# Delta-rule layer on one core: ScalarE's decays behind the copy of the state, its first taps of the values behind the next rounding

## The chip, the cores and the metric

The kernel runs on one core of a Trainium2 chip. The metric is the device time of one execution in microseconds, as the median of several runs. One profiled execution gives the trace; times "at 1205" and the like are microseconds from the start of its span. The engines: TensorE (PE in the rows; PEld are its weight loads), VectorE (DVE), ScalarE (ACT), GpSimd (POOL) and SyncE (SP), which issues the loads of the weights. Each runs its own instructions in order and waits on semaphores.

## What is computed

The reference is a block of two layers (one of retention, one of the gated delta rule, each beside an attention to a memory), followed by a second block of pooling, HGRN and an MLP, for 256 tokens of width 2048 in float32. The change touches the layer of the delta rule alone:

```python
qkv = silu(conv4(h[..., :CONV_CH], conv_w))       # causal, 4 taps
q, k = l2_normalised(qkv[...]), ...               # 12 heads of 128; v has 24
beta = sigmoid(b); g = -exp(a_log) * softplus(a + dt_bias)
g_cum = cumsum(g)                                 # over a chunk
decay = tril(exp(g_cum[i] - g_cum[j]))
lower = strict_tril((k * beta) @ k.T * decay)
u, w = solve(I + lower, [v * beta, k * beta * exp(g_cum)])
# per chunk, in order of time:
v_new = u_i - w_i @ state
out = q_i @ state + (q_i @ k_i.T * decay) @ v_new
state = state * exp(g_last) + k_tail.T @ v_new
```

The kernel computes it with two chunks of 128 tokens, called tile 0 and tile 1. So there is one state to be carried over, from tile 0 to tile 1, and it starts from zero.

## The kernel before

**Units and halves.** Nearly all the work of TensorE is products of the activations with weights that stream in from memory. They are cut into units of 2048 x 512 weights (or 512 x 2048 for the output), and a unit into 8 halves, q = 0 to 7, of 256 x 512. To keep float32's precision on TensorE each half is split in a high part `whi`, which ScalarE rounds (`half`, line 1080), and a low part `wlo = raw - whi`, which GpSimd computes in two instructions (line 440). TensorE then does 12 matmuls on the half (lines 496 to 498). There are four buffers for halves: ScalarE rounds half q only when TensorE has done half q-4, and GpSimd and TensorE follow in order. GpSimd does nothing but this.

**A group of the delta rule.** The layer runs over 6 groups of 4 value heads (2 heads of q and k). A group has a unit for q and k, one for v, one for the gate z, and from group 1 on one for the output projection of the group before. Groups 2 to 5 stand in a loop of two bodies; groups 0 and 1 are written out ahead of it, group 0 without the output's unit and with its later steps spread over its z unit in another way (`first_places`).

**Steps.** Everything that isn't a weight product is placed between the halves. After each half q of a unit, ScalarE calls `gdn_steps(g, n, ...)` for the numbers n that belong there: in the unit of q and k first n = 32 + q of the group before, then n = q of this group (`in_qk`); in the unit of v 40 + q and 8 + q; in the unit of z 48 + q and 16 + q (`in_z`); in that of the output 24 + q. TensorE has numbers of the same kind and its own steps (`gdn_run`, `gdn_v`, `gdn_level_p`). ScalarE is three to four halves ahead of TensorE, so the same number doesn't mean the same time. VectorE runs one list without halves.

**What stands around the first move.** In the unit of q and k of group g:
- n = 36 (q = 4) of group g-1: ScalarE scales tile 0's new values (`vn0`, line 1477), which TensorE uses for tile 0's output (`o0`).
- then, still behind q = 4, the decays of group g (lines 1409 to 1421): eight ACTIVATEs with Abs, a drain, and one Exp, for which the activation table is loaded anew. They write `dn`, and end with the semaphore `decay_ready`. VectorE uses them in `gdn_decay` (line 2043) and for the lower triangles.
- n = 37 (q = 5) of group g-1: the copy of the state out of PSUM (`copy_out` of "st", line 1131), which TensorE's next step needs (`from_state`, line 741), and `out_squares(g-1, 0)` (line 1386), which first waits for VectorE's gate of tile 0 (line 2144).
- n = 39 (q = 7): the copy of tile 1's new values; n = 40 and 41 in the unit of v: `out_squares(g-1, 1)` and, behind the next half, the square root of the mean squares (line 1488), which waits for VectorE's line 2175; n = 42: the scaling of the output (line 1493).

VectorE, in the same stretch: tile 0's gate (2144), the new values with the state (2150), tile 1's sum and gate (2157 to 2162), seven small copies of the next group's parameters (2028, 2035 to 2037), `gdn_decay` (2043), the mean squares (2175), the reciprocal (2172), then the turning of q and k (1862).

**Around the second move.** In the unit of z, n = 18: ScalarE copies v out of PSUM (`wide_out`), TensorE turns it (line 555, `gdn_v`), n = 21 (q = 5): `first_tap` of both halves of v (line 1373) starts the convolution, which VectorE goes on with (line 2018) after `gdn_lower` (lines 2051 to 2089) and a small copy (2121). n = 22 (q = 6): `merge` of the triangles for the levels of the inverse. VectorE's `gdn_base` (2097 to 2116) ends the triangles' base with line 2111, and TensorE's first level (line 712) waits for that. In group 0 n = 21 stands behind the z unit's half 4 and n = 22 behind half 5.

Of the kernel before, what the change touches and what calls it, by code (L numbers as in the profile page):

```python
# [119 lines left out]
def fill(phase, step, g=0):  # L120

    for bank in range(4):
        before = 0
        for name, rounds, steps in PHASES:
            if name == phase and step in steps[bank]:
                return bank, g * len(steps[bank]) + (before + steps[bank].index(step) + 1)
            before += rounds * len(steps[bank])
    raise KeyError((phase, step))
# [29 lines left out]
def build(nc, x_in, mem_in, pos_in, w_ret, ret_g, w_gdn, conv_w, a_log, dt_bias, gdn_g, w_kv, w_out,  # L158
# [6 lines left out]
    with ExitStack() as ctx:  # L165
# [906 lines left out]
        def _(act):  # L1072
# [35 lines left out]
            def wide_out(m, pair, func, dst, norm=None, taken=None):  # L1108

                act.wait_ge(sub_used, 8 * m + 8)  # L1110
                if taken is not None:
                    act.wait_ge(wide_taken, 2 * taken)
                for t in range(TT):
                    scale = 1.0 if norm is None else inverse_rms(norm)[:, t:t + 1]
                    act.activation(dst(t), acc[pair][t][:, :], func, scale=scale).then_inc(wide_taken, 1)
# [4 lines left out]
            def tiles(buf):  # L1120
                return lambda t: buf[:, t * COL:(t + 1) * COL]
# [220 lines left out]
            def is_first(g):  # L1342
                return isinstance(g, int) and g == 0
# [23 lines left out]
            def first_tap(dst, tile, step, g):  # L1367

                b, n = fill("gdn", step, g)
                act.wait_ge(filled[b], n)  # L1370
                for k in range(2):
                    c = slice(((tile + k) % 4) * SEQ, ((tile + k) % 4 + 1) * SEQ)
                    op = act.activation(dst[:, c], bank[b][:, k * SEQ:(k + 1) * SEQ], ACT.Copy,
                                        scale=small[:, 88 + tile + k:89 + tile + k])
                return op
# [25 lines left out]
            def gdn_steps(g, n, at, pair):  # L1401
                if n == (8 if is_first(g) else 0):
# [3 lines left out]
                        act.wait_ge(s["decay_ready"], g)  # L1406
                    src = log_decays[:, ds(4 * g, 4), :].partition_broadcast(P)
                    act.dma_start(cb[:, 0:1024].rearrange("p (t h c) -> p t h c", t=TT, h=4), src).then_inc(s["rows_here"], 16)
                if n == (11 if is_first(g) or isinstance(g, int) and g == 1 else 4):
                    if not is_first(g):  # L1410
                        b, c = fill("gdn", "n64", g - 1)
                        act.wait_ge(filled[b], c)
                    act.wait_ge(s["rows_here"], 16 * g + 16)
                    for t in range(TT):
                        for hh in range(4):
                            c = slice(t * COL + hh * P, t * COL + (hh + 1) * P)
                            at_g = TT * NVH + t * NVH + hh
                            bias = gates[:, at_g:at_g + 1] if is_first(g) else gates[:, ds(4 * g + at_g, 1)]
                            act.activation(dn[:, c], cb[:, c], ACT.Abs, scale=-1.0, bias=bias)
                    act.drain()  # L1420
                    act.activation(dn[:, :], dn[:, :], ACT.Exp, scale=-1.0).then_inc(s["decay_ready"], 1)
# [21 lines left out]
                if n == 18:  # L1443
# [1 line left out]
                        b, c = fill("gdn", "o1", g - 1)  # L1445
                        act.wait_ge(filled[b], c)
                    wide_out(at + 1, 1 - pair, ACT.Copy, tiles(n1), taken=W_GDN + 3 * g + 1)
                if n == 21:
                    first_tap(sq, 4, "va", g).then_inc(s["conv_begun"], 1)
                    first_tap(sq, 6, "vb", g).then_inc(s["conv_begun"], 1)  # L1450
                if n == 22:
# [176 lines left out]
            def gate_sums(q):  # L1628
# [11 lines left out]
                act.activation(gates[:, 4 * n48:5 * n48], n1[:, 288:336], ACT.Exp).then_inc(s["gate_step"], 1)  # L1640

            layer(U_GDN, W_GDN, B_L1, gdn_steps, "gdn", "att1", gate_steps, spread_first=True)
            act.wait_ge(s["branch_ready"], 2 * BR)
            ln_rows(1)
# [1079 lines left out]
```

## Time and profile before

| | |
|---|---|
| median of 3 runs | 2769.76 us (2769.64 to 2771.84) |
| profiled execution, its own time | 2771.87 us |
| its span | 2770.1 us |
| TensorE busy | 2742.0 us (99%) |
| GpSimd busy | 2342.9 us (85%) |
| ScalarE busy | 1380.4 us (50%) |
| VectorE busy | 1301.9 us (47%) |
| TensorE's granted clock, mean | 0.997 of 2.4 GHz |

The layer of the delta rule with its attention lies at about 860 to 1690 us of the span; the group that is looked at most runs from 1192 to 1300. A line of a timeline gives the start, the length, engine, line, operation, what it writes and reads, and in brackets how long the engine was idle before it and what ended that. "x6" after the shapes means that six such instructions are merged in one row. Busy times of TensorE are modelled at their ends, so it is the starts of its matmuls that are compared.

### The profile page before, as it was taken

The numbers are of one execution on the slowest core, as the hardware profiler recorded it, in microseconds if no ns is written. First come the engines' busy times: TensorE is split into PE (matmuls) and PEld (weight loads), VectorE is DVE, ScalarE is ACT, GpSimd is POOL, SyncE is SP. The second block draws the span as 40 slices with busy tenths as digits, with TensorE's granted clock in tenths as the row PEclk, the third lists the DMA queues.
The fourth block names the chain that finished last, engine by engine and source line by source line (L and its number), as shares of the span: only waits on it lengthen the run. The fifth ranks groups of instructions, "written<-read, shape, count | busy, mean of one in ns | idle before, by whom it ended". The sixth has DMA issues, their size and how long they took to land.

```text
span 2770.1 us, 38752 instructions
## 1 busy us (share of the span) xinstructions
PE 2742.0 (99%) x12719; PEld 2280.6 (82%) x12719; DVE 1301.9 (47%) x2729; ACT 1380.4 (50%) x1843; POOL 2342.9 (85%) x1831
## 2 busy tenths in 40 slices
PE   8999999999999999999999999999999999999998
PEld 7888888888888888888888887888878888888886
DVE  5232234224663576856757465646253323233234
ACT  4444444444444665665655545655445444444444
POOL 8988898888889867876877787888789999999997
PEclk9999999999999999999999999999999999999999
DMA  8555565555566544554545455555556556565653
GB/s 287 189 185 184 186 198 186 182 186 172 178 228 196 174 140 160 170 161 157 168 159 167 152 175 190 168 167 181 180 169 196 184 194 197 185 198 192 197 189 130
DMA packets 284354, 502.67 MB, mean 181 GB/s; under 512 B 18021, under 2 KB 68662, under 8 KB 283190
## 3 DMA queue, kind: packets, MB, share of 16 engines
q1 hardware_dynamic: 275606, 482.55, 53.4%
q10 hardware_dynamic: 8608, 18.24, 1.8%
q8 instruction: 89, 1.46, 0.2%
q14 instruction: 51, 0.42, 0.0%
HBM read 498.61 MB, written 2.12 MB: 181 GB/s over the span
## 4 chain that ended last, share of the span: by engine, by line
POOL 54%; PE 24%; issue 21%; POOLq 1%; DVE 0%; DVEq 0%; ACT 0%
POOL wlo L440 54%; PE acc L496 8%; PE acc L498 8%; PE acc L497 8%; POOLq L438 0%; POOLq L435 0%; DVE x_sb L2510 0%; DVE big L2486 0%; POOLq L440 0%; DVE kv L1914 0%; DVEq L165 0%; ACT small L1502 0%; DVE small L2477 0%; POOL eps_sb L434 0%; DVE small L2503 0%
## 5 line engine op out<-in xcount | busy, mean ns | idle before, releaser
L440 POOL TENSOR_TENSOR wlo<-raw,whi 128x512 fp32r<-128x512 f32 x1824 | 2342.4, 1316 | 410.0 <-ACT whi L1080 393.6
L1080 ACT ACTIVATE whi<-raw 128x1024 fp32r<-128x1024 f32 x910 | 958.3, 1060 | 1076.2 <-PE acc L498 1034.8
L496 PE MATMUL acc<-whi,a_lo 128*128 128x512 f32 x2528 | 999.5, 395 | 3.1 <-POOL wlo L440 2.4
L498 PE MATMUL acc<-whi,a_hi 128*128 128x512 f32 x2528 | 984.9, 390 | 0.0
L497 PE MATMUL acc<-wlo,a_hi 128*128 128x512 f32 x2528 | 984.3, 389 | 0.0
L496 PEld LDWEIGHTS acc<-whi,a_lo 128*128 128x128 f32 x2528 | 474.9, 188 | 103.4 <-POOL wlo L440 4.4
L498 PEld LDWEIGHTS acc<-whi,a_hi 128*128 128x128 f32 x2528 | 474.4, 188 | 100.1
L497 PEld LDWEIGHTS acc<-wlo,a_hi 128*128 128x128 f32 x2528 | 475.0, 188 | 96.4 <-issue 1.4
L496 PE MATMUL acc<-whi,b_lo 128*128 128x512 f32 x928 | 365.5, 394 | 0.0
L498 PE MATMUL acc<-whi,b_hi 128*128 128x512 f32 x928 | 361.3, 389 | 0.0
L497 PE MATMUL acc<-wlo,b_hi 128*128 128x512 f32 x928 | 361.3, 389 | 0.0
L1914 DVE TENSOR_TENSOR kv<-acc,kv 128x512 f32<-128x512 f32 x160 | 103.2, 686 | 415.9 <-PE acc L498 415.9
L1862 DVE STREAM_TRANSPOSE bank<-br 32x256 f32<-32x256 f32 (+1 forms) x544 | 235.4, 438 | 10.3 <-issue 2.3
L498 PEld LDWEIGHTS acc<-whi,b_hi 128*128 128x128 f32 x928 | 174.2, 188 | 36.5
L497 PEld LDWEIGHTS acc<-wlo,b_hi 128*128 128x128 f32 x928 | 174.4, 188 | 34.8
L496 PEld LDWEIGHTS acc<-whi,b_lo 128*128 128x128 f32 x928 | 174.4, 188 | 34.7
L1914 DVE TENSOR_TENSOR x_sb<-acc,x_sb 128x512 f32<-128x512 f32 x128 | 82.5, 685 | 159.3 <-PE acc L498 159.3
L462 PE MATMUL acc<-whi,a_hi 128*128 128x512 f32 x192 | 79.5, 414 | 2.1 <-ACT a_hi L1143 1.8
L463 PE MATMUL acc<-wlo,a_hi 128*128 128x512 f32 x192 | 77.5, 404 | 0.0
L1814 DVE TENSOR_TENSOR a_lo<-bank,a_hi 128x512 fp32r<-128x512 f32 x32 | 20.7, 685 | 88.8 <-ACT a_hi L1140 88.8
L1961 DVE TENSOR_TENSOR big<-bank,big 128x256 f32<-128x256 f32 x12 | 5.1, 425 | 112.3 <-PE bank L615 111.9
L470 PE MATMUL acc<-whi,a_lo 128*128 128x512 f32 x192 | 52.0, 393 | 0.0
(307 smaller groups left out, 2007.7 us busy)
## 6 DMA issues: line engine op xcount, KB each, us to landing
raw<-in_w_in_ret SPq DMA_DIRECT2D x176, 512.0 KB, 4.4
raw<-in_w_in_gdn SPq DMA_DIRECT2D x176, 512.0 KB, 4.3
raw<-in_w_out SPq DMA_DIRECT2D x160, 512.0 KB, 4.5
raw<-in_w_mlp_in SPq DMA_DIRECT2D x128, 512.0 KB, 4.4
raw<-in_w_mlp_out SPq DMA_DIRECT2D x128, 512.0 KB, 4.3
raw<-in_w_in SPq DMA_DIRECT2D x80, 512.0 KB, 4.5
raw<-in_w_mem_kv SPq DMA_DIRECT2D x63, 512.0 KB, 4.8
cb<-log_decays ACTq DMA_DIRECT2D x6, 512.0 KB, 5.1
```

The source lines that it names most:

```text
L440: part = pool.tensor_tensor(wlo[q % 4][:, c], raw_half[:, c], whi[q % 4][:, c].bitcast(f32), ALU.subtract)
L462: pe.matmul(acc[pair][t][:, :], a_hi[:, at:at + P], w_h, start=start and block == 0, stop=False)
L463: pe.matmul(acc[pair][t][:, :], a_hi[:, at:at + P], w_l, start=False, stop=False)
L470: mm = pe.matmul(acc[pair][t][:, :], a_lo[:, at:at + P], w_h, start=False, stop=stop and block == KB - 1)
L496: pe.matmul(dst, l, w_h, start=start and block == 0, stop=False)
L497: pe.matmul(dst, h, w_l, start=False, stop=False)
L498: mm = pe.matmul(dst, h, w_h, start=False, stop=stop and block == KB - 1)
L1080: act.activation(whi[q % 4][:, :], raw[j][:, (q % 2) * HALF:(q % 2 + 1) * HALF], ACT.Copy).then_inc(hi_ready, 1)
L1814: op = tt(lo, b[:, :], hi, SUB)
L1862: last = dve.transpose(squares(dst, "b t")[32 * j:32 * (j + 1), blocks, :, 32 * i:32 * (i + 1)], squares(src, "t b")[32 * i:32 * (i + 1), ...
L1914: tt(to, acc[(pair + j) % 2][t][:, :], to, ADD).then_inc(out_added, 1)
L1961: tt(pi[:, to:to + SEQ], b[:, 0:SEQ], dec, MUL)
```

## The change

Two numbers in `gdn_steps` of ScalarE. The decays of group g move from behind half 4 (and n = 36 of the group before) to behind half 5 (and n = 37 of the group before: the copy of the state and the squares of tile 0's output). This holds for groups 2 to 5; groups 0 and 1 keep them behind n = 11. The first taps of the values move behind the rounding of the next half, ahead of the wait for the triangles, in all six groups.

```diff
-                if n == (11 if is_first(g) or isinstance(g, int) and g == 1 else 4):
+                if n == (11 if is_first(g) or isinstance(g, int) and g == 1 else 5):
                     if not is_first(g):
                         b, c = fill("gdn", "n64", g - 1)
                         act.wait_ge(filled[b], c)
...
-                if n == 21:
+                if n == 22:
                     first_tap(sq, 4, "va", g).then_inc(s["conv_begun"], 1)
                     first_tap(sq, 6, "vb", g).then_inc(s["conv_begun"], 1)
                 if n == 22:
```

## Rows read from the trace of the kernel before

**Rows 1.** The page, part 1: busy time, share of the span, instructions.

```profile
PE 2742.0 (99%) x12719; PEld 2280.6 (82%) x12719; DVE 1301.9 (47%) x2729; ACT 1380.4 (50%) x1843; POOL 2342.9 (85%) x1831
```

**Rows 2.** TensorE's waits, 1085 to 1480 us: who for whom, total, times, longest.

```profile
PE bank L741 <- ACT st L1131: 0.9, 4, 0.2
```

**Rows 3.** Timeline of ScalarE, 1192 to 1302: start, length, instruction, [idle before, releaser].

```profile
1200.73 2.44 ACT L1419 ACTIVATE big<-cb,gates 128x128 f32<-128x128 f32 x8
...
1205.48 1.04 ACT L1080 ACTIVATE whi<-raw 128x1024 fp32r<-128x1024 f32 x1
...
1206.43 0.58 ACT L1131 ACTIVATE st<-bank 128x512 f32<-128x512 f32 x1
...
1206.91 0.27 ACT L1386 ACTIVATE sq<-bank 128x128 f32<-128x128 f32 x1
...
1208.23 2.01 ACT L1080 ACTIVATE whi<-raw 128x1024 fp32r<-128x1024 f32 x2 [0.19 <-issue]
...
1221.67 0.21 ACT L1488 ACTIVATE scales<-scales 128x8 f32<-128x8 f32 x1
...
1221.78 1.04 ACT L1080 ACTIVATE whi<-raw 128x1024 fp32r<-128x1024 f32 x1
...
1225.08 2.00 ACT L1080 ACTIVATE whi<-raw 128x1024 fp32r<-128x1024 f32 x2
...
1256.19 1.57 ACT L1373 ACTIVATE sq<-bank,small 128x256 f32<-128x256 f32 x4 [3.02 <-PE bank L555]
```

**Rows 4.** Timeline of GpSimd, the same stretch.

```profile
1209.37 7.58 POOL L440 TENSOR_TENSOR wlo<-raw,whi 128x512 fp32r<-128x512 f32 x6 [0.25 <-ACT whi L1080]
...
1220.43 5.04 POOL L440 TENSOR_TENSOR wlo<-raw,whi 128x512 fp32r<-128x512 f32 x4 [3.48 <-ACT whi L1080]
```

**Rows 5.** Timeline of VectorE, the same stretch.

```profile
1204.30 0.69 DVE L2144 TENSOR_TENSOR br<-bank,zs 128x512 f32<-128x512 f32 x1 [2.73 <-PE bank L734]
...
1217.86 0.18 DVE L2028 COPY small<-gates 128x48 f32 x1
...
1218.38 1.22 DVE L2043 TENSOR_TENSOR big<-big,cst 128x1024 f32<-128x1024 f32 x1
...
1219.51 0.16 DVE L2175 SCALAR_TENSOR_TENSOR scales<-small,scales 128x8 f32<-128x8 f32 x1
```

**Rows 6.** Timeline of TensorE, 1206.5 to 1208 and 1226.6 to 1230.5.

```profile
1206.55 0.39 PE L498 MATMUL acc<-whi,a_hi 128*128 128x512 f32 x1
...
1207.15 1.10 PE L741 MATMUL bank<-st,cv 128*128 128x256 f32 x4 [0.22 <-ACT st L1131]
...
1227.17 0.39 PE L496 MATMUL acc<-whi,a_lo 128*128 128x512 f32 x1
...
1229.89 0.39 PE L496 MATMUL acc<-whi,a_lo 128*128 128x512 f32 x1
```

**Rows 7.** Timelines from 43 to 59 us; then two lines' instructions (ns min/median/max).

```profile
51.52 7.76 DVE L2417 SCALAR_TENSOR_TENSOR gates<-big,gates 128x128 f32<-128x128 f32 x6
...
42.44 16.69 POOL L440 TENSOR_TENSOR wlo<-raw,whi 128x512 fp32r<-128x512 f32 x13
...
L2088 DVE TENSOR_TENSOR big<-near,cst x6: 419/1506/1520, 954.8 to 1469.8; 128x256 f32<-128x256 f32 x6
...
L2121 DVE COPY inv<-cst x6: 188/1280/1284, 955.1 to 1471.2; 128x64 f32<-128x64 f32 x6
```

**Rows 8.** Timelines of ScalarE, GpSimd, VectorE, TensorE in group 0, 948 to 968.5.

```profile
953.23 1.57 ACT L1373 ACTIVATE sq<-bank,small 128x256 f32<-128x256 f32 x4 [2.96 <-PE bank L555]
...
948.53 6.01 POOL L440 TENSOR_TENSOR wlo<-raw,whi 128x512 fp32r<-128x512 f32 x4 [1.56 <-ACT whi L1080]
...
955.83 5.05 POOL L440 TENSOR_TENSOR wlo<-raw,whi 128x512 fp32r<-128x512 f32 x4 [1.28 <-ACT whi L1080]
...
966.34 0.67 DVE L2111 STREAM_TRANSPOSE big<-big 128x512 f32<-128x512 f32 x1
...
967.99 0.72 PE L712 MATMUL bank<-big,n 128*128 128x128 f32 x5
```

## The prediction, made before the changed kernel was run

> **What bounds the kernel now.** I read the page's first part, then the waits of TensorE, then the four engines' timelines over one group of the loop. TensorE is busy 99% of a span of 2770.1 us [rows 1], and over the four groups that the change reaches in the loop its longest wait in total is the one for ScalarE's copy of the state, four times 0.2, 0.9 us in all [rows 2]. So almost nothing can be gained: a change can only take away this wait, or make new ones. All that it moves lies on ScalarE, VectorE and GpSimd, beside TensorE, and the question is whether one of them becomes late for it.
>
> The link is the chain of halves. ScalarE rounds a half of a weight block (`half`, two in 2.01 us), GpSimd takes the low part in two instructions (six in 7.58 us, 1.26 us each, the first 1.14 us behind the half's start [rows 3, 4]), and TensorE runs 12 matmuls on it, 2.72 us from one half to the next [rows 6]. I write qk5, v2 or z5 for half 5, 2 or 5 of a group's unit of q and k, of v, or of z. The group at 1192 to 1300 us stands for the four of the loop.
>
> **Part 1, the decays.** Eight ACTIVATEs, a table load and an Exp go from behind qk4 to behind qk5 and the two steps that stand there. They last from 1200.73 to the start of qk5 at 1205.48, 4.75 us [rows 3]. Nothing is added or removed. Moved are:
> - qk5, to about 1200.8; TensorE comes to it past 1212, so there is no gain in that by itself.
> - The copy of the state, from 1206.43 to about 1203.1, when TensorE has just filled the bank. The matmuls on the state no longer wait: 0.22 us by the row, 0.37 if they follow the last big matmul (1206.55) at the usual 0.23 instead of at 1207.15 [rows 6]. I take 0.37.
> - The squares of tile 0's output. They now wait for VectorE's gate, over at 1204.99 [rows 5], and take 1.32 us, as before between their start (1206.91) and the next half (1208.23) [rows 3]: over at 1206.3.
> - The decays then run to 1211.1, so qk6 starts at 1211.1 instead of 1208.23, 2.9 us late, and qk7 and v0 behind it. GpSimd has their six instructions from 1212.2 to 1219.8 instead of 1209.37 to 1216.95 [rows 4]. Counted back from v3 in steps of 2.72 [rows 6], and 0.37 earlier, TensorE starts qk6 at 1215.9 and v0 at 1221.4; their parts are there at 1214.7 and 1219.8. Up to here every delay is covered, by 1.2 us.
>
> What is late next is VectorE. At 1217.86 it begins seven small copies, then the product of the decays with the triangle, 1.22 us, and the mean squares (L2175), over at 1219.67 [rows 5]. Today this falls into the gap in which GpSimd is idle, 1216.95 to 1220.43 [rows 4]; afterwards GpSimd is busy there. What that does is in the trace: at 51.52 six small VectorE operations of 128x128 take 7.76 us, 1.29 each, while GpSimd runs 13 instructions back to back in 16.69 us, 1.28 each. The two alternate, one operation of VectorE for each of GpSimd. The copy of 64 columns (L2121) takes 1280 ns in most groups and 188 in the one where GpSimd is idle; L2088 takes 1506 against 419 [rows 7]. I take this price for the small copies too, since L2121 is the nearest row.
>
> The Trainium skill says why (SBUF — State Buffer, "SBUF: two separate sides"): VectorE's operations with two SBUF inputs or in a two-port mode and GpSimd's share one port pair, an exclusive lock held for a whole instruction. The trace agrees, with the 1280 against 188 ns. It is the rule that speaks against this change; by the same page ScalarE and TensorE never wait for that port, and by that alone the moved work would cost nothing and the time would be that of my second rival.
>
> Step by step, with TensorE 0.37 us ahead: VectorE comes to its copies at 1217.5; GpSimd holds on until 1218.5; first copy; GpSimd's last instruction for v0 until 1219.8; second copy. The other copies last 0.07 us each, to about 1220.2, but v1's parts are now ready at 1220.43 - 0.37 = 1220.06, so GpSimd gets in again, to 1221.3, and after one more copy again, to 1222.6. Then the remaining copies (0.2), the product (1.1) and L2175: 1224.1 instead of 1219.67. ScalarE's square root behind them starts at 1221.67 today, held only by its table load [rows 3]; now it waits to 1224.1, 2.4 us. Behind it are queued v2, the scaling of the output, v3 and v4: v2 starts at 1224.2 instead of 1221.78, v3 3.30 us behind it, at 1227.5 instead of 1225.08. Low parts: v2 1225.3 to 1227.8; v3 1228.7 to 1231.2. TensorE began v2 at 1227.17 and v3 at 1229.89 [rows 6]; now v3 begins at 1231.3, **1.4 us late**. v4's low parts are there at 1233.7 against 1234.0, so nothing is added after that, and TensorE, which has no idle time, never recovers it. Four groups: +5.6 us. Bounds for one group: -0.37 if the port is no hindrance, and +2.5 if the 2.4 us by which VectorE is late also reach the triangles (third rival).
>
> **Part 2, the first taps of the values.** They go behind z6's rounding. In the loop ScalarE idles 3.02 us before the taps at 1256.19 [rows 3], until TensorE has turned v, while z6 needs only z2's matmuls, which end just before that turning; so z6 is rounded in the end of the idle time and the taps start about 0.5 us later. VectorE takes the first two up after L2121, at about 1257.7, when they are done, and GpSimd is busy around L2121 already [rows 7]: covered, 0 us. **Group 0 differs**: there ScalarE idles 2.96 us before the taps at 953.23, and z5's rounding comes after them, so GpSimd is idle from 954.54 to 955.83 while VectorE does L2088 and L2121 in 0.42 and 0.19 us [rows 8]. With the taps behind z5, that half is rounded at about 952.8 and GpSimd goes on at 954.54 without a gap. L2088 and L2121 then cost what they cost in the loop, 1.51 and 1.28 us [rows 7]: 2.2 us more. The triangles' base ends (L2111) at 967.01 [rows 8] and would end at 969.2. TensorE's first level (L712), at 967.99 today, waits for it, to about 969.35: **+1.35 us**, once. Bounds: 0 (VectorE gets through before GpSimd's next instruction) and 2.2.
>
> **Sum.** 4 x 1.4 + 1.35 = 6.95, say +7.0 us: the profiled span goes from 2770.1 to 2777.1, that execution from 2771.87 to 2778.9, and the median of the runs, which is 2.1 us under that execution, from 2769.76 to **2776.8 us**, 0.25% slower.
>
> **Rivals.**
> 1. *VectorE keeps its turn through the copies.* If GpSimd's v1 comes after the product has begun (the two are 0.2 us apart: 1220.06 against 1220.27), L2175 waits for one instruction of v1, not two, and the chain ends at 1222.8. v2 then starts at 1223.0 and v3 at 1226.3, and TensorE is 0.16 us late a group: +0.6 + 1.35 = +2.0, 2771.8 us. For it: the margin is small. Against it: TensorE's gain of 0.37 us brings v1 forward, and makes the collision.
> 2. *Not slower: the port is no hindrance to such small operations.* Copies of 4 to 48 columns with a computed address are in no contended row of the loop. Then only the wait for the state goes: 4 x -0.37 = -1.5, and nothing in group 0: 2768.3 us. Against it: L2121 is a small copy as well, and waits.
> 3. *Worse: the late VectorE is also late for the triangles.* It turns q and k, convolves, turns the output, and with that ScalarE's rounding of the output (L1177) and the square root for the keys come up to 1.0 us later than TensorE has become, and L2111 has 1.4 us of room before TensorE's first level. Contention could use that up: up to 1.0 more a group, +4, 2780.8 us.
> 4. *The order changes nothing*, because ScalarE would wait at the same places: 2769.8. Against it: 4.75 us of work pass a half that is ready.
>
> **How the numbers follow.** Forecast 0.57, rival 1 0.19, rival 2 0.12, rival 3 0.09, rival 4 0.03. About 0.2% (5.5 us) is what a measurement of this kernel can tell from no change: slower is above 2775.3, faster below 2764.2. Slower: rival 3 and most of the forecast (it ends under 2775.3 if one group in the sum costs 1.0 rather than 1.4), 0.47 + 0.09 = 0.56. Faster: no case reaches it, 0.02. The rest, 0.42. The range for 8 in 10 leaves out rival 2 and the upper end of rival 3: 2769.2 to 2780.0; forecast alone: 2774.0 to 2778.5.
>
> **What would show it.** In the loop: no wait of L741 for the copy of the state; qk6's rounding 2.9 us later against qk4; the small copies (L2035 to L2037), L2043 and L2175 longer than 0.16, 1.22 and 0.16 us, one or more near 1.3; ScalarE's L1488 waiting for L2175; a TensorE wait for `wlo` at v2 or v3. In group 0: L2088 and L2121 near 1.5 and 1.3 us, a TensorE wait at L712. It is wrong if the copies stay at 0.16 us, if GpSimd has a gap there after all, or if TensorE's new waits stand elsewhere.

## The result, and the profile after

The changed kernel takes 2777.62 us in the median of 10 runs (2775.32 to 2778.82), the kernel before 2769.82 in the median of 10 runs taken with them (2768.04 to 2771.84). The ratio is 1.0025, with a 95% interval of 1.0017 to 1.0034, so the change costs 4.7 to 9.4 us. The forecast was 2776.8. The profiled execution has a span of 2774.7 us and took 2776.48, against 2770.1 and 2771.87 before.

The page, part 1: busy time, share of the span, instructions.

```profile
PE 2742.0 (99%) x12719; PEld 2278.3 (82%) x12719; DVE 1322.2 (48%) x2729; ACT 1379.5 (50%) x1843; POOL 2344.6 (84%) x1831
```

TensorE's work is the same to 0.1 us [rows 1], so the time is waiting. ScalarE, whose order was changed, is busy 0.9 us less. The engine that nobody touched, VectorE, is busy 20.3 us longer with the same 2729 instructions: they have become longer.

TensorE's waits, 900 to 1530 us (for whom, total us, times, longest):

```profile
PE acc L496 <- POOL wlo L440: 3.9, 8, 0.7
PE bank L712 <- issue: 1.3, 2, 0.9
PE acc L496 <- DVE x_sb L1914: 0.8, 1, 0.8
```

The wait of L741 for the copy of the state [rows 2] is gone. In its place TensorE waits for low parts twice a group, eight times in all, and at L712.

ScalarE's timeline, 1192 to 1262 us. TensorE begins this group 1.44 us later than before (its L734 at 1200.06 instead of 1198.62), so times of before are compared with 1.44 added.

```profile
1204.75 0.60 ACT L1131 ACTIVATE st<-bank 128x512 f32<-128x512 f32 x1 [1.51 <-PE bank L757]
1206.47 0.28 ACT L1386 ACTIVATE sq<-bank 128x128 f32<-128x128 f32 x1 [1.12 <-DVE br L2144]
...
1207.97 2.45 ACT L1419 ACTIVATE big<-cb,gates 128x128 f32<-128x128 f32 x8 [0.36 <-issue]
...
1212.74 1.99 ACT L1080 ACTIVATE whi<-raw 128x1024 fp32r<-128x1024 f32 x2
...
1221.36 1.28 ACT L1488 ACT_TABLE_LOAD   x1
1225.16 0.21 ACT L1488 ACTIVATE scales<-scales 128x8 f32<-128x8 f32 x1 [2.52 <-DVE scales L2175]
1225.28 1.04 ACT L1080 ACTIVATE whi<-raw 128x1024 fp32r<-128x1024 f32 x1
...
1228.56 2.94 ACT L1080 ACTIVATE whi<-raw 128x1024 fp32r<-128x1024 f32 x3
```

qk6 is rounded at 1212.74, 3.07 us later than 1208.23 + 1.44 [rows 3]. The square root (L1488) had no idle time before it in [rows 3]; now ScalarE stands 2.52 us for VectorE's L2175, with v2 and v3 queued behind.

GpSimd, then VectorE, in the same stretch:

```profile
1213.86 10.11 POOL L440 TENSOR_TENSOR wlo<-raw,whi 128x512 fp32r<-128x512 f32 x8 [8.04 <-ACT whi L1080]
...
1226.40 2.54 POOL L440 TENSOR_TENSOR wlo<-raw,whi 128x512 fp32r<-128x512 f32 x2 [2.43 <-ACT whi L1080]
```

```profile
1218.84 0.18 DVE L2028 COPY small<-gates 128x48 f32 x1
1218.93 1.31 DVE L2035 COPY small<-cols 128x4 f32 x1
1220.16 0.16 DVE L2036 COPY small<-cols 128x4 f32 x1
1220.23 1.27 DVE L2037 COPY small<-cols 128x8 f32 x1
1221.41 0.16 DVE L2035 COPY small<-cols 128x4 f32 x1
1221.49 1.26 DVE L2036 COPY small<-cols 128x4 f32 x1
1222.66 0.16 DVE L2037 COPY small<-cols 128x8 f32 x1
1222.73 2.32 DVE L2043 TENSOR_TENSOR big<-big,cst 128x1024 f32<-128x1024 f32 x1
1224.98 0.15 DVE L2175 SCALAR_TENSOR_TENSOR scales<-small,scales 128x8 f32<-128x8 f32 x1
```

These rows show the mechanism; whether it is the cause is tested below. GpSimd's gap from 1216.95 to 1220.43 [rows 4] is closed: eight instructions run back to back to 1223.97. In that stretch three copies of four to eight columns take 1.26 to 1.31 us, and the product (L2043) 2.32 instead of 1.22 [rows 5]. The two groups behind this one have the same lengths to 0.02 us. In the first group of the loop four copies wait and the product doesn't:

```profile
1110.59 1.32 DVE L2028 COPY small<-gates 128x48 f32 x1
1111.84 1.32 DVE L2035 COPY small<-cols 128x4 f32 x1
...
1115.65 1.21 DVE L2043 TENSOR_TENSOR big<-big,cst 128x1024 f32<-128x1024 f32 x1
```

Either way it is about 4.5 us more a group, 17.8 in four, and with the 2.2 of group 0 (below) it is the 20 us of the page. L2175 ends at 1225.13 instead of 1219.67 + 1.44 = 1221.11. Since ScalarE then rounds v2 late, GpSimd has a gap of 2.43 us, and TensorE waits for v2 and v3, its first matmuls on them (1228.0 to 1232.5):

```profile
1228.99 0.50 PE L496 MATMUL acc<-whi,a_lo 128*128 128x512 f32 x1 [0.67 <-POOL wlo L440]
...
1232.28 0.50 PE L496 MATMUL acc<-whi,a_lo 128*128 128x512 f32 x1 [0.28 <-POOL wlo L440]
```

By starts, the first stands 1.06 us and the second 0.67 us behind the matmul before it, where 0.23 is usual. TensorE was ahead before that, by 0.45 us and not by 0.37: its wait for the state is gone (0.38 from L734 to L741), and the step behind L741 takes 0.68 us instead of 0.75 (1208.21 to 1208.89, against 1207.15 to 1207.90). So v3 should start 0.83 + 0.10 + 0.44 - 0.45 = 0.92 us late (the 0.10 is the slower step behind a wait, 0.33 instead of 0.23). Measured from L734 it is (1232.28 - 1200.06) - (1229.89 - 1198.62) = 0.95.

For the rest of this document three lengths are worked out from the traces: **groups**, from one group's scaling of tile 0's new values (L1477) on ScalarE to the next group's, first for group 0 to 1 and so on to 4 to 5; **g0**, in group 0 from TensorE's turning of v (L555) to its first level (L712); and **layer**, from one layer's L2382 to the next's, with the whole delta rule in between.

| kernel | groups, us | g0 | layer |
|---|---|---|---|
| before | 94.50, 107.07, 107.70, 107.06, 107.07 | 15.40 | 883.07 |
| after | 94.53, 108.25, 109.22, 108.19, 108.17 | 16.71 | 889.40 |

After minus before: +1.18, +1.52, +1.13, +1.10 in the four groups of the loop, 4.93 in all, and +1.31 in group 0. These two make 6.24 of the layer's 6.33.

### The profile page after: what moved, and what is told of

Read it like the earlier page. It is cut to its first block, busy times and chain, and to the rows that moved or that the text cites. A ratio compares the mean times of both kernels' runs of the same rounds, so it can differ in the third digit from the quotient of the medians.

```text
span 2774.7 us, 38752 instructions
## 1 busy us (share of the span) xinstructions
PE 2742.0 (99%) x12719; PEld 2278.3 (82%) x12719; DVE 1322.2 (48%) x2729; ACT 1379.5 (50%) x1843; POOL 2344.6 (84%) x1831
## 4 chain that ended last, share of the span: by engine, by line
POOL 54%; PE 24%; issue 21%; POOLq 1%; DVE 0%; DVEq 0%; ACT 0%
POOL wlo L440 54%; PE acc L496 8%; PE acc L497 8%; PE acc L498 8%; POOLq L438 0%; POOLq L435 0%; DVE x_sb L2510 0%; POOLq L440 0%; DVE big L2486 0%; DVE kv L1914 0%; DVEq L165 0%; ACT small L1502 0%; DVE small L2477 0%; POOL eps_sb L434 0%; DVE small L2503 0%
## 5 line engine op out<-in xcount | busy, mean ns | idle before, releaser
L440 POOL TENSOR_TENSOR wlo<-raw,whi 128x512 fp32r<-128x512 f32 x1824 | 2344.1, 1318 | 412.7 <-ACT whi L1080 396.6
L1914 DVE TENSOR_TENSOR kv<-acc,kv 128x512 f32<-128x512 f32 x160 | 103.2, 686 | 416.0 <-PE acc L498 416.0
L1862 DVE STREAM_TRANSPOSE bank<-br 32x256 f32<-32x256 f32 (+1 forms) x544 | 235.3, 438 | 10.3 <-issue 2.3
L1914 DVE TENSOR_TENSOR x_sb<-acc,x_sb 128x512 f32<-128x512 f32 x128 | 82.5, 685 | 159.4 <-PE acc L498 159.4
```

The source lines that it names most:

```text
L440: part = pool.tensor_tensor(wlo[q % 4][:, c], raw_half[:, c], whi[q % 4][:, c].bitcast(f32), ALU.subtract)
L1862: last = dve.transpose(squares(dst, "b t")[32 * j:32 * (j + 1), blocks, :, 32 * i:32 * (i + 1)], squares(src, "t b")[32 * i:32 * (i + 1), ...
L1914: tt(to, acc[(pair + j) % 2][t][:, :], to, ADD).then_inc(out_added, 1)
```

## Experiments

The theory: the new waits come from the SBUF ports that VectorE's copies and GpSimd share, as the prediction has it ("the port" from here on); ScalarE's own new order costs nothing and even gives the 0.4 us a group of the wait for the state. The rivals: ScalarE's order makes the halves late by itself (late qk6, longer wait for the gate), and part 2 has a share in the loop too. The kernel before was timed again beside the variants: 2771.34 us beside the first four, 2770.12 beside the rest.

### Each part alone

The decays alone move (the taps are put back):

```diff
-                if n == 22:
+                if n == 21:
                     first_tap(sq, 4, "va", g).then_inc(s["conv_begun"], 1)
```

> Only the decays go behind half 5; the first taps stay where they were. Theory (port): all of the loop's loss is the decays': GpSimd's instructions for half 6 to v0 come to lie on VectorE's small copies, the two alternate, L2175 ends some 4 us later, ScalarE's square root waits 2.5 us and TensorE waits twice for wlo in each of four groups. A group of the loop takes 1.1 to 1.5 us more than in the kernel before (107.07 and once 107.70 us), 4.9 us in all, and group 0 is as before (15.4 us from the turning of v, L555, to the first level, L712). Median 2774.7 us. Rival (the taps' place costs in the loop too, since it shifts ScalarE's halves there): a group takes less than 1.0 us more, and the median is under 2773.

Measured: ratio 1.0016 (1.0007 to 1.0025), 2776.02 against 2771.34 us. Groups 94.52, 108.21, 109.05, 108.26, 108.18; g0 15.40; layer 887.88, 4.81 over before. Its waits of TensorE, 900 to 1600 us:

```profile
PE acc L496 <- POOL wlo L440: 4.4, 9, 0.7
...
PE bank L712 <- issue: 0.4, 1, 0.4
```

The taps alone move:

```diff
-                if n == (11 if is_first(g) or isinstance(g, int) and g == 1 else 5):
+                if n == (11 if is_first(g) or isinstance(g, int) and g == 1 else 4):
```

> Only the first taps go behind the next half's rounding. Theory (port): the loop's groups stay at 107.07 and 107.70 us; in group 0 L2088 and L2121 take 1.5 and 1.3 us instead of 0.42 and 0.19, TensorE waits 0.9 to 1.0 us at L712, and from L555 to L712 it is 16.7 us instead of 15.4. Median +1.3: 2771.1 us. Rival (group 0's loss comes from the later taps, not from GpSimd's earlier start): L2121 stays at 0.19 us and line 2018 starts late for another reason.

Measured: ratio 1.0007 (0.9998 to 1.0016), 2772.91 against 2771.34. Groups 94.51, 107.07, 108.12, 107.10, 107.05; g0 16.72, which is 1.32 over before; layer 884.94, 1.87 over. Its waits of TensorE, 900 to 1600 us, and its VectorE and GpSimd in group 0:

```profile
PE bank L712 <- issue: 1.3, 2, 0.9
...
PE bank L741 <- ACT st L1131: 0.9, 4, 0.2
```

```profile
953.81 1.51 DVE L2088 TENSOR_TENSOR big<-near,cst 128x256 f32<-128x256 f32 x1
955.25 1.27 DVE L2121 COPY inv<-cst 128x64 f32<-128x64 f32 x1
```

```profile
947.52 11.62 POOL L440 TENSOR_TENSOR wlo<-raw,whi 128x512 fp32r<-128x512 f32 x8 [1.56 <-ACT whi L1080]
```

The two parts are independent and stand where the prediction put them: the waits for `wlo`, two a group, come with the decays (the ninth lies at the third interval's end, where the kernel before has one too), the wait at L712 in group 0 with the taps. In the loop the taps cost nothing in three of the four intervals. The other 0.4 of this kernel's 1.87 is in the third group's interval; that one varies in every kernel, and comes up again below. The two excesses over before, 4.81 and 1.87, make 6.68, the changed kernel has 6.33. The interval of the taps alone includes no change: 1.3 us of 2770 can be seen in a trace and hardly in a ratio.

### The port, or ScalarE's order?

If the order on ScalarE is the cause, then the cost stays when VectorE's copies are done elsewhere. Here both parts of the change stay, and only VectorE's list is altered, so that the six copies (L2035 to L2037) of a group of the loop stand ahead of tile 1's sum, where VectorE is idle and so is GpSimd:

```diff
-                    if not first:
+                    if first:
+                        gdn_group(g)
+                        gdn_taps(g)
+                    else:
+                        gdn_taps(g)
                         gdn_sum(g - 1)
-                    gdn_group(g)
-                    gdn_taps(g)
+                        gdn_group(g)
```

> Both edits, and VectorE's six copies of the taps (gdn_taps) stand ahead of gdn_sum, where it waits for TensorE and GpSimd is idle; three of the nine small operations (L2028, L2043, L2175) stay. Theory (port): six operations fewer to alternate with; L2175 ends about 2.3 us earlier than with the change, before ScalarE's table load is over, the square root waits under 0.3 us, TensorE's waits for wlo in the loop go, a group takes 106.7 to 107.1 us and group 0's 1.3 us stay. Median 2770 us. Rival (ScalarE's own lateness, 2.9 us for halves 6 to v0, is the cause, and VectorE's only follows from it): the groups stay at 108.2 and the median at 2777.

Measured: ratio 0.9999 (0.9990 to 1.0008), 2770.52 against 2771.34. Groups 94.53, 106.68, 107.35, 106.64, 106.63; g0 16.70; layer 882.90. Its waits of TensorE, then VectorE's timeline, 1206 to 1227 us:

```profile
PE bank L712 <- issue: 1.3, 2, 0.9
...
PE acc L496 <- POOL wlo L440: 0.4, 1, 0.4
```

```profile
1209.36 0.16 DVE L2035 COPY small<-cols 128x4 f32 x1
...
1217.97 2.36 DVE L2043 TENSOR_TENSOR big<-big,cst 128x1024 f32<-128x1024 f32 x1
1220.25 1.25 DVE L2175 SCALAR_TENSOR_TENSOR scales<-small,scales 128x8 f32<-128x8 f32 x1
```

The same copies take 0.16 us each. A group of the loop falls from 108.2 to 106.65, 0.4 **below** before. The product and the mean squares still wait for one GpSimd instruction each (2.36 and 1.25 us), but L2175 ends at 1221.50, in time for the square root: its table load is over at 1221.67, so the margin is 0.17 us. The halves are as late as with the change: qk6 is rounded at 1211.77, 3.46 us behind the start of VectorE's L2150, as in after, while before it came 0.06 ahead of it. So ScalarE's order costs nothing, and what costs lies in the copies. But the move also takes the copies out of that stretch as work, not only as waits. The next run leaves them in place and takes only the port away.

### The same copies, in the same place, without the port

```diff
-                    dve.tensor_copy(taps[:, :, 0:2], src[:, :, ds(2 * g, 2)])
+                    dve.tensor_reduce(taps[:, :, 0:2], src[:, :, ds(2 * g, 2)].unsqueeze(3), AX.X, ADD)
```

and so for the other two of `gdn_taps`: a sum over an axis of length one, which writes the same values.

> Both edits; the six copies of the taps stay where they are, but are sums over an axis of length one (TENSOR_REDUCE), the same numbers and places. A TENSOR_REDUCE ran beside GpSimd without being stretched in the kernel before (L2082). Theory (port): an operation that needs no shared port doesn't take turns, so each lasts 0.15 to 0.3 us beside a busy GpSimd, L2175 ends about 2.3 us earlier than with the change and the group takes 106.7 to 107.2 us; median about 2770. Rival (any small VectorE operation waits for GpSimd, or the place in time is what counts): they take 1.3 us each as the copies do, and the median stays at 2777.

Measured: ratio 0.9996 (0.9987 to 1.0006), 2769.95 against 2771.34. Groups 94.54, 106.67, 107.23, 106.65, 106.65; g0 16.72; layer 882.82. VectorE and GpSimd, 1206 to 1230 us:

```profile
1217.75 0.18 DVE L2028 COPY small<-gates 128x48 f32 x1
1217.84 0.15 DVE L2035 TENSOR_REDUCE small<-cols 128x4 f32 x1
...
1218.17 0.16 DVE L2037 TENSOR_REDUCE small<-cols 128x8 f32 x1
1218.23 1.97 DVE L2043 TENSOR_TENSOR big<-big,cst 128x1024 f32<-128x1024 f32 x1
1220.12 1.25 DVE L2175 SCALAR_TENSOR_TENSOR scales<-small,scales 128x8 f32<-128x8 f32 x1
```

```profile
1212.76 17.35 POOL L440 TENSOR_TENSOR wlo<-raw,whi 128x512 fp32r<-128x512 f32 x13 [8.04 <-ACT whi L1080]
```

Same place, same count, same sizes, beside a GpSimd that is busy all through, and 0.15 to 0.16 us each: what the copies waited for was not GpSimd's work in general but a resource that one form of instruction takes and the other doesn't. The Trainium skill has this (SBUF — State Buffer, "Who interferes with whom"): a copy can take the pair of ports that VectorE shares with GpSimd, `tensor_reduce` on this chip never. The traces agree, with 1.31 against 0.15 us on the same four columns.

It isn't always VectorE that waits. L440 in the same stretch of this run (ns, min/median/max):

```profile
L440 POOL TENSOR_TENSOR wlo<-raw,whi x13: 1276/1292/2265, 1212.8 to 1228.8; 128x512 fp32r<-128x512 f32 x13
```

One GpSimd instruction takes 2.27 us instead of 1.29. It is the one that starts at 1219.08, when the product (L2043, until 1220.20) has had its turn. With the change none of the eight is longer than 1.30.

### Where the gain of 0.37 us a group comes from

The copies early, once with the decays moved and the taps not, once in the kernel before with neither. Both diffs are against the kernel before:

```diff
-                if n == (11 if is_first(g) or isinstance(g, int) and g == 1 else 4):
+                if n == (11 if is_first(g) or isinstance(g, int) and g == 1 else 5):
...
+                        gdn_taps(g)
                         gdn_sum(g - 1)
-                    gdn_group(g)
-                    gdn_taps(g)
+                        gdn_group(g)
```

> Only the decays behind half 5, and the six copies of the taps ahead of gdn_sum; the first taps as in the kernel before. Theory (port): the change's gain is left alone: no wait for the copy of the state (0.22 to 0.37 us a group), no wait for wlo, and group 0 at 15.4 us. Groups of the loop 106.6 to 106.9 us, the layer 1.0 to 1.5 us shorter than before; median 1 to 1.5 us under the kernel before, which the timing can hardly tell from none. Rival (the late halves 6 to v0 cost something of their own): groups at 107.07 or more.

```diff
+                        gdn_taps(g)
                         gdn_sum(g - 1)
-                    gdn_group(g)
-                    gdn_taps(g)
+                        gdn_group(g)
```

> The kernel before with only the six copies moved ahead of gdn_sum. Theory (port): before, GpSimd was idle when the copies ran, so moving them does nothing: groups of 107.07 us and once 107.7, TensorE's wait for the state stays. Rival (the copies' new place is a gain by itself, and not through the port): groups get shorter here too, by 0.2 us or more.

Measured for the first: ratio 0.9999 (0.9990 to 1.0008), 2770.38 against 2770.12; groups 94.54, 106.68, 107.61, 106.66, 106.64; g0 15.40; layer 881.79. For the control, one execution and no ratio: 2769.66 us; groups 94.54, 107.07, 108.21, 107.12, 107.08; layer 883.67. TensorE's waits in the first and in the control:

```profile
PE acc L496 <- POOL wlo L440: 0.6, 1, 0.6
```

```profile
PE bank L741 <- ACT st L1131: 0.9, 4, 0.2
```

The early copies alone give nothing: three groups are within 0.06 us of before, and the wait for the state stays. With the decays moved they give 0.39 to 0.43 us in three groups: this is the wait for the state, which the forecast had at 0.37. The medians (2770.38 against 2770.12) don't show it. That the copies would be as cheap there as in their old place didn't hold: in the control they fall beside a busy GpSimd, and three of them again take about 1.3 us (1.31, 1.25, 1.25, every second one). VectorE comes 1.2 us late to L2157 (4.81 us behind the start of L2150 instead of 3.63), but idles 2.70 us ahead of the next, L2160, and so nobody waits. So VectorE can pay for a collision without TensorE being late: what matters is who waits for VectorE next.

### Group 0: the same remedy

After L2088, VectorE makes the small copy L2121, which nothing needs before the base. It is moved ahead of the lower triangles, once in the changed kernel and once together with the early copies:

```diff
             def gdn_mid(g, adds):
-                gdn_lower(g)
                 dve.tensor_copy(rows, spread(place, 8))
+                gdn_lower(g)
```

> Both edits as in the change; the copy into inv (L2121) stands ahead of gdn_lower, where VectorE waits for ScalarE. Theory (port): in group 0 only L2088 still takes its turn behind GpSimd; line 2111 ends 1.1 us late instead of 2.2, TensorE's wait at L712 is under 0.3 us instead of 0.87, and L555 to L712 takes 15.4 to 15.7 us. The loop stays as with the change, groups at 108.2. Rival (what delays group 0 is the order on ScalarE, the taps behind half 5): 16.7 us stay.

> Both edits with both moves of copies (the taps' six ahead of gdn_sum, inv's ahead of gdn_lower). Theory (port): the losses of both places are gone, the groups of the loop 106.6 to 106.9 us, group 0 at 15.4 to 15.7, the layer 1 us shorter than before or better, median 1 to 1.5 us under the kernel before. Rival: as for the other two, 1 us or more above it.

Measured for the first (one execution, 2774.82 us): groups 93.89, 108.20, 109.54, 108.19, 108.18; g0 15.69; layer 888.00. For both moves: ratio 0.9995 (0.9986 to 1.0004), 2769.45 against 2770.12; groups 93.84, 106.69, 107.37, 106.63, 106.64; g0 15.69; layer 881.16. The first one's waits of TensorE and its VectorE and TensorE in group 0:

```profile
PE acc L496 <- POOL wlo L440: 3.8, 8, 0.7
```

```profile
954.43 1.52 DVE L2088 TENSOR_TENSOR big<-near,cst 128x256 f32<-128x256 f32 x1
955.88 5.09 DVE L2018 SCALAR_TENSOR_TENSOR sq<-bank,small,sq 128x255 f32<-128x255 f32 x12
```

```profile
955.60 0.39 PE L498 MATMUL acc<-whi,a_hi 128*128 128x512 f32 x1
956.01 1.13 PE L697 MATMUL bank<-big,cst 128*128 128x512 f32 x2
956.57 0.79 PE L496 MATMUL acc<-whi,a_lo 128*128 128x512 f32 x1
```

g0 falls from 16.71 to 15.69: of the 1.31 us that part 2 cost, 1.02 came through this one copy of 64 columns. The rest, 0.29, is in the last rows, TensorE's in the same group: L697, its first step on the triangles, starts when L2088 is over (954.43 + 1.52 = 955.95) and 0.41 behind the matmul before it, where 0.23 is usual, and the step behind it takes 0.56 instead of the 0.45 of before: 0.18 + 0.11. All TensorE waits at L712 are gone, one in group 1 among them that the kernel before has as well (0.4 by its row), and the first interval is 0.6 shorter than in the kernels with the copy in its old place. That was not foreseen. By starts that wait is longer than its row: in before L712 stands 0.78 us behind the matmul ahead of it (1055.96 and 1056.74), with the copy moved 0.23 (1055.87 and 1056.10). These 0.55 us and the slower step behind a wait make up the 0.6.

The last kernel has both parts of the change, nearly none of their costs, and the shortest layer of all: 881.16 us, 1.9 under before. Over the whole program that is 0.07%, and its interval, 0.14% faster to 0.04% slower, can't tell it from no change. By the trace it is the best of these kernels, and by its times it is equal to before.

## Why the prediction was right, step by step

- **TensorE bound, nothing but 0.37 us a group to be gained.** Right. The wait for the state went, and with the collision removed (the decays with the copies early) a group is 0.39 to 0.43 shorter. In after, TensorE is 0.45 ahead when it comes to v2: the term is 0.08 too small, since the step behind the wait gets shorter too.
- **qk6 late by 2.9 us and covered.** 3.07 late, and TensorE shows no wait before v2.
- **VectorE comes to its copies at 1217.5.** In before's time it does at 1218.84 - 1.44 = 1217.40. GpSimd runs through from there, until 1223.97 - 1.44 = 1222.53; the working had 1222.6.
- **Every contended operation waits for one GpSimd instruction.** Half right, and the term that was mis-sized. The working had four copies wait, and then the rest of the copies (0.2 us) and the product (1.1) behind the last of GpSimd's. In the trace of three of the four groups tiny copies pass behind one that waited (0.18, 1.31, 0.16, 1.27, 0.16, 1.26, 0.16), so three copies and the product are the four that wait, and no copy is left behind the end of GpSimd. Only in the first group of the loop do four copies wait. Both ways four instructions are waited for, since their number is set by GpSimd's stretch. L2175 then ends at 1225.13 - 1.44 = 1223.69 instead of 1224.1.
- **ScalarE's square root waits 2.4 us; v2 from 1224.2, v3 from 1227.5.** It starts at 1225.16 - 1.44 = 1223.72, which is 2.05 later than before. The 2.4 was such a delay as well; the idle time is 2.52, because the table load is over 0.47 earlier than before. v2 from 1223.84, v3 from 1227.12. These 0.4 us less are the point before, handed on.
- **TensorE begins v3 1.4 us late.** 0.95, by the same 0.4. The intervals of the groups have +1.18, +1.13 and +1.10 in the three others, since the second wait leaves a slower matmul step behind it as well, of 0.10 us, and the working had neither of the two. With +1.52 in the third group the loop costs 4.93 where the sum had 5.6.
- **Part 2 costs nothing in the loop, and 1.35 in group 0.** 1.31 (1.32 alone). L2088 and L2121 take 1.52 and 1.26 where 1.51 and 1.28 were taken over from the loop. The total hides a missed step: the working had only L712 waiting, while L697 waits for L2088 as well (0.29), and L712 then adds 1.02.
- **Rival 1**, VectorE keeps its turn: refuted, GpSimd's eight instructions, v1's two among them, run on until 1223.97, 1.2 us past the start of the product's row (1222.73), so the product comes behind both of v1's. **Rival 2**, no hindrance for small operations: refuted by four columns at 1.31 us. **Rival 3**, the triangles late as well: the lateness is there (ScalarE's rounding of the output, L1177, waits 1.05 us for VectorE's L1862 at 1247.03), but TensorE waits at no L712 of the loop. **Rival 4** fell with the first row of waits.

VectorE's and TensorE's rows in group 0 of after, for the last but one point and for the size of that wait (timelines, 952 to 969):

```profile
953.63 1.52 DVE L2088 TENSOR_TENSOR big<-near,cst 128x256 f32<-128x256 f32 x1
955.08 1.26 DVE L2121 COPY inv<-cst 128x64 f32<-128x64 f32 x1
...
967.36 0.67 DVE L2111 STREAM_TRANSPOSE big<-big 128x512 f32<-128x512 f32 x1
```

```profile
968.13 1.13 PE L712 MATMUL bank<-big,n 128*128 128x128 f32 x8 [0.87 <-issue]
```

The 4.93 and the 1.31 are sums within one profiled execution. The medians differ by 7.8 us, which the 6.3 of the layer doesn't reach; the interval of 4.7 to 9.4 has room for both. The spans of the two profiled executions differ by 4.6 us only, so outside the layer after is 1.7 us shorter. The traces show where, in places that the change doesn't touch. At the start TensorE's matmuls stand 0.43 us apart until 12.03 us in before and until 10.21 in after, and then 0.23; when the layer begins (L2382) after is 1.19 ahead, 806.48 against 807.67. Behind the layer, after two idle times of TensorE of 0.8 to 0.9 us, the granted clock from 1694 to 1700 us is 0.72 of 2.4 GHz in before, with matmuls 0.43 us apart again, the pace of the lower level of 1.2 GHz; in after it is 1.00 from 1694 to 1710. The same stretch of TensorE's work takes 10.79 us in before (L572, 1692.95 to 1703.74) and 9.84 in after (1698.09 to 1707.93). The mean granted clock also varies from one execution to the next: of the ten of after, seven have a mean granted clock of 0.997 and take 2778.1 us on average, three have 0.998 and take 2776.1. Whether the 1.5 us by which the medians differ more than the layer come from this is not shown. So the forecast's closeness to the median (0.8 us) is partly luck: by the traces its sum of 7.0 was 0.7 too large.

**What stays open.** The interval of the third group is 0.6 to 1.35 us longer than its neighbours in every kernel, the one before included: there lies the loop's back edge, and TensorE waits for VectorE's L1914 or for a low part. In after:

```profile
1303.72 0.49 PE L496 MATMUL acc<-whi,a_lo 128*128 128x512 f32 x1 [0.75 <-DVE x_sb L1914]
```

The extra goes from about 0.6 (before) to 1.1 (the taps alone, the control) and 1.35 (the change with L2121 early), in no order that the edits explain, so 0.4 of the loop's 4.93 may be noise of that place. An order of VectorE's in which L2175 comes ahead of the copies, and another form of L2175, weren't tried.

## To carry to other kernels

When work moves on one engine, ask what that fills on another: here eight ACTIVATEs of ScalarE moved by one half closed a gap of GpSimd's, and it was that gap in which VectorE's smallest copies had been cheap. A copy of four columns costs 0.16 us beside an idle GpSimd and up to 1.3 beside a busy one, so price a VectorE list by the number of GpSimd instructions that its operations can wait for, at most one each, and not by the operations' size: here eight operations waited four times, because GpSimd had four instructions left. Then look at who waits for the end of the list. The cheap remedies are to put such copies where both engines are idle, or to write them in a form that doesn't take the port.

## Not expected of the hardware

- The alternation isn't one for one with tiny copies. After a copy that has waited 1.25 to 1.32 us one to three more take 0.16 us (one each time in the group shown of after and in the control: 1.31, 0.16, 1.25, 0.16, 1.25; three once with the decays alone). It isn't a fixed pattern: in the first group of the loop two copies in a row wait 1.32 us each. Other operations waited each time: L2043 and then L2175, which is 8 columns wide, took 2.36 and 1.25 us, and the six of 128x128 1.29 each [rows 7]. What decides is not shown.
- GpSimd can be the one that waits: with the copies early or as sums, one of its instructions takes 2.27 us instead of 1.29 while VectorE's product runs. Its busy time in the page is 2347.5 us there (sums) and 2344.6 in after, and TensorE doesn't wait for it.
- A sum over an axis of length one costs the same 0.15 to 0.16 us as the copy that it replaces, and isn't held up.
- The table load of the square root runs ahead of the wait of its ACTIVATE: in after it starts at 1221.36 and ends at 1222.64, and only then do 2.52 us of idle time follow. L2175 ends at 1225.13 and the square root starts at 1225.16: behind that wait there is no load left to be paid.
